# Gated heads of a two-layer decoder step: sample states in a buffer of their own, updates in groups, norm and gates in the next head

## What is computed

```python
def gla_step(s, q, k, v, la):
    bcum = jnp.cumsum(la, axis=1)
    qt = q * jnp.exp(bcum)
    kt = k * jnp.exp(-bcum)
    a = jnp.where(causal, jnp.einsum('bqhd,bshd->bhqs', qt, kt), 0.0)
    o = jnp.einsum('bhqs,bshe->bqhe', a, v) + jnp.einsum('bqhd,bhde->bqhe', qt, s)
    blast = bcum[:, -1]
    k_dec = k * jnp.exp(blast[:, None] - bcum)
    s_new = jnp.exp(blast)[..., None] * s + jnp.einsum('bshd,bshe->bhde', k_dec, v)
    return s_new, o
...
    ob = rms_norm(ob, gla_g).astype(x.dtype).reshape(b, length, W_B)
    mixed = jnp.concatenate([oa * jax.nn.silu(ga), ob * jax.nn.silu(gb)], axis=-1)
```

## Time and profile before

| | us |
|---|---|
| median of 3 runs | 3133.46 (3132.65 to 3137.24) |
| the profiled execution | 3134.93 |
| its span, first to last instruction | 3133.4 |
| PE busy in it | 2939.4 (94%) |
| DVE busy | 1125.1 (36%) |
| ACT busy | 870.7 (28%) |
| DMA queues, mean | 141 GB/s |

### The profile page before, as it was taken

The page is one execution under the profiler, slowest core; times in us unless marked ns, Lnnn a source line. Parts: engine busy times, 40 slices in busy tenths (PEclk is TensorE's granted clock), DMA queues, the critical chain, the costliest instruction groups (busy, mean ns, idle before and its releaser), DMA issues.

```text
span 3133.4 us, 52698 instructions
## 1 busy us (share of the span) xinstructions
PE 2939.4 (94%) x22412; PEld 2712.8 (87%) x22412; DVE 1125.1 (36%) x1589; ACT 870.7 (28%) x1353; POOL 239.3 (8%) x386
## 2 busy tenths in 40 slices
PE   4599997988989898999999999999999999999998
PEld 3388886977978898989899898989989898899998
DVE  1244442232232535334234342433434243443422
ACT  1244343232321322223223132322313232221221
POOL 1020000000000000001010100101010010110111
PEclk7699997988989999999999999999999999999999
DMA  9954431645655343434252533425253443565442
GB/s 308 306 172 123 127 115 43 202 147 155 197 153 160 117 132 108 119 118 150 88 169 83 181 91 119 150 81 174 84 172 96 128 138 104 171 188 168 114 134 65
DMA packets 525769, 442.64 MB, mean 141 GB/s; under 512 B 12320, under 2 KB 491958, under 8 KB 525025
## 3 DMA queue, kind: packets, MB, share of 16 engines
q1 hardware_dynamic: 485664, 300.30, 33.5%
q0 software_dynamic: 39920, 139.52, 12.8%
HBM read 370.39 MB, written 72.51 MB: 141 GB/s over the span
## 4 chain that ended last, share of the span: by engine, by line
PE 86%; DMA 5%; DVE 4%; ACT 2%; issue 1%; POOL 0%; SPq 0%; DVEq 0%; ACTq 0%; POOLq 0%
PE PJ L1458 65%; PE AD L1506 3%; DMA W_raw<-in_ada_w_even 2%; PE X L1440 2%; PE X L1902 2%; PE X L1896 2%; PE PJ L1477 1%; PE X L1869 1%; PE X L1847 1%; PE X L1838 1%; PE X L1477 1%; DMA work<-in_state_gla 1%; DMA out<-work 1%; PE X L1499 1%; PE PJ L1493 1%
## 5 line engine op out<-in xcount | busy, mean ns | idle before, releaser
L1458 PE MATMUL PJ<-act_hi,W_hi 128*128 128x272 f32 x5600 | 1637.1, 292 | 10.2 <-issue 7.3
L1458 PE MATMUL PJ<-act_lo,W_hi 128*128 128x272 f32 x5600 | 1619.2, 289 | 0.0
L1458 PE MATMUL PJ<-act_hi,W_lo 128*128 128x272 f32 x5600 | 1618.2, 289 | 0.0
L1458 PEld LDWEIGHTS PJ<-act_hi,W_hi 128*128 128x128 f32 x5600 | 1061.5, 190 | 47.8 <-issue 41.5
L1458 PEld LDWEIGHTS PJ<-act_lo,W_hi 128*128 128x128 f32 x5600 | 1061.5, 190 | 2.7
L1458 PEld LDWEIGHTS PJ<-act_hi,W_lo 128*128 128x128 f32 x5600 | 1059.2, 189 | 0.0
L997 DVE TENSOR_TENSOR W_lo<-W_raw,W_hi 128x2048 fp32r<-128x2048 f32 x183 | 419.1, 2290 | 488.3 <-ACT W_hi L603 487.7
L603 ACT ACTIVATE W_hi<-W_raw 128x2048 fp32r<-128x2048 f32 x183 | 349.0, 1907 | 249.0 <-PE PJ L1458 231.6
L619 ACT ACTIVATE tiles<-PJ 128x272 f32<-128x272 f32 x222 | 88.2, 397 | 1048.2 <-PE PJ L1458 1033.8
L1355 DVE SCALAR_TENSOR_TENSOR W_raw<-W_raw,work,X 128x512 f32<-128x512 f32 x128 | 90.0, 744 | 144.1 <-PE X L1847 144.1
L1506 PE MATMUL AD<-W_raw,cs 128*32 128x256 f32 x1280 | 93.8, 443 | 27.4 <-DMA W_raw<-in_ada_w_even 27.4
(11 more groups left out here) (355 smaller groups left out, 2579.6 us busy)
## 6 DMA issues: line engine op xcount, KB each, us to landing
W_raw<-in_w_in_odd SPq DMA_DIRECT2D x96, 1024.0 KB, 6.1
W_raw<-in_ada_w_even SPq DMA_DIRECT2D x24, 2048.0 KB, 8.8
W_raw<-in_ada_w_odd SPq DMA_DIRECT2D x24, 2048.0 KB, 8.3
W_raw<-in_w_in_even SPq DMA_DIRECT2D x42, 1024.0 KB, 11.3
W_raw<-in_state_ret POOLq DMA_DIRECT2D x64, 512.0 KB, 7.2
out<-W_raw POOLq DMA_DIRECT2D x64, 512.0 KB, 3.2
W_raw<-in_w_out_odd SPq DMA_DIRECT2D x32, 1024.0 KB, 6.4
W_raw<-in_w_out_even SPq DMA_DIRECT2D x16, 1024.0 KB, 6.2
```

The costliest lines, as they stand in the source:

```text
L1458: last = mm(PJ[:, c, 0:HALF], w[:, par, k], x[:, k, c * HALF:(c + 1) * HALF], start=(k == 0 and a == 0), stop=(k == KT - 1 and a == 2))
```

## The change

- The sample states get a buffer of their own (`SST`, in the upper quarter of `W_raw`). POOL loads the states of the next head as soon as those of this one are stored, and no longer stores, waits and loads between the prompt's and the samples' part.
- The modulation slab keeps the other quarter: 1 MB (`hslab`). It is loaded twice per product, its first half used before the product's first half, its second between the product's halves. A new semaphore `ad_half` tells SP when the first is used. The select moves into the middle of the product's second half.
- Sample outputs (`sample_rows`) stand after the first quarter of the sixth product, the prompt's outputs after the second, and the state products in two groups of four after the third and the fourth. There are four mask buffers, and each PSUM bank takes two products. DVE masks and updates by fours; the last four updates and the sum of squares (`gla_tail`) come in the next head.
- The norm's sum (`gla_norm`) is taken after the first quarter of the next head's first product, or inside the paired product of the output projection behind the last head; the root (`gla_rstd`) and the gates follow there. The first sigmoid is made during the sixth product, the second in the next head. PE no longer waits for the root.
- ACT makes the high part of the next head's second weight at the end of a head; DVE copies the low-rank weights one head ahead.
- The loops of the output projections and of retention heads 1 to 7 are written out on all engines. The modulation loop at the start stays.

```diff
-        BVS, BKM = STK[0:3 * NS, 0:256], STK[0:3 * NS, 512:768].rearrange("p (a b) -> p a b", a=2)
+        BVS, BKM = STK[0:3 * NS, 0:256], STK[0:3 * NS, 256:768].rearrange("p (a b) -> p a b", a=4)
+        hslab = WR[:, 4096:6144].rearrange("p (k n) -> p k n", k=8)
+        SST = WR[:, 6144:8192].rearrange("p (b e) -> p b e", b=NB)
+        N1 = u(5512, T)
...
-                for j in range(6):
-                    load(h * 6 + (N_B + j), (N_B + j) % 2, wie[:, :, src[j]])
-                    ada_pair(h * 6 + (24 + j), ao, h * 1536 + 256 * j)
...
+            gla_weight(0)
+            for i in range(6 * HB):
+                if i + 1 < 6 * HB:
+                    gla_weight(i + 1)
+                else:
+                    load(N_W0, N_W0 % 2, woe[:, :, 0:128])
+
+                sp.wait_ge(s["ad_done"], 24 + i)
+                sp.dma_start(hslab, ao[:, 0:8, 256 * i:256 * i + 256]).then_inc(adl[1], 16)
+                sp.wait_ge(s["ad_half"], i + 1)
+                sp.dma_start(hslab, ao[:, 8:16, 256 * i:256 * i + 256]).then_inc(adl[1], 16)
...
-                wait_for(s["b_o"], h * 2 + 2)
-                pool.dma_start(ST, I["state_gla"][0][:, ds(h, 1)].rearrange("b h p e -> p (b h) e")).then_inc(s["b_sld"], 16)
-                wait_for(s["b_sup"], h * 8 + 8)
-                pool.dma_start(O[8][0][:, ds(h, 1)].rearrange("b h p e -> p (b h) e"), ST).then_inc(s["b_stf"], 16)
-                wait_for(s["b_stf"], h * 16 + 16, "b_free")
+                if h > 0:
+                    pool.wait_ge(s["b_stf"], 16 * h)
+                pool.dma_start(SST, I["state_gla"][0][:, h:h + 1].rearrange("b h p e -> p (b h) e")).then_inc(s["b_sld"], 16)
+                pool.wait_ge(s["b_st"], 8 * h + 8)
+                pool.dma_start(O[4][0, 0, h:h + 1].rearrange("h p e -> p (h e)"), ST[:, 7]).then_inc(s["b_pst"], 16)
+                pool.wait_ge(s["b_sup"], 8 * h + 8)
+                pool.dma_start(O[8][0][:, h:h + 1].rearrange("b h p e -> p (b h) e"), SST).then_inc(s["b_stf"], 16)
...
+            def gla_rstd(h):
+                act.wait_ge(s["b_ms"], h + 1)
+                link(A(halves(N1), X[:, 2:4, 0:HALF], ACT.Ln, bias=eps[:, 0:1], scale=1.0 / 256))
+                A(N1, N1, ACT.Exp, scale=-0.5).then_inc(s["b_rb"], 1)
...
+                gla_evac(4, R3[:, 8 + 2 * h])
+                gla_sigmoid(h, 0)
+                evac(n + 5, 0, R3[:, 9 + 2 * h, 0:HALF])
+                act.wait_ge(s["b_so"], h + 1)
...
+                evac(n + 5, 1, R3[:, 9 + 2 * h, HALF:T])
+                split_hi(n + 7, 0)
...
+                        if k == 2:
+                            gla_sigmoid(HB - 1, 1)
+                        if k == 5:
+                            gla_rstd(HB - 1)
...
+            def gla_silu(h, e):
+
+                dve.wait_ge(s["b_eg"], 2 * h + e + 1)
+                g = R3[:, 8 + 2 * h + e]
+                TT(g, g, T1, ALU.mult).then_inc(s["b_gate"], 1)
+
+            def gla_gate(h):
+
+                dve.wait_ge(s["b_rb"], 3 * h + 3)
+                for e in range(2):
+                    g = R3[:, 8 + 2 * h + e]
+                    link(STT(BP[:, 2 + e], BP[:, 2 + e], vecT2[:, 16 + e:17 + e], N1, ALU.mult, ALU.mult))
+                    dve.wait_ge(s["b_gate"], 4 * h + 2)
+                    TT(g, g, BP[:, 2 + e], ALU.mult).then_inc(s["b_gate"], 1)
...
+            def masked_keys(h, b0):
+                for b in range(b0, b0 + 4):
+                    TS(BKM[:, b % 4], BKS, bmask[0:3 * NS, b:b + 1], None, ALU.mult).then_inc(s["b_kdm"], 1)
+
+            def new_states(h, b0):
+                for b in range(b0, b0 + 4):
+                    at = 256 * (b % 4 // 2)
+                    STT(SST[:, b], SST[:, b], ebl[:, 8 + b:9 + b], X[:, 2 + b % 2, at:at + 256], ALU.mult, ALU.add).then_inc(s["b_sup"], 1)
+
+            def gla_tail(h):
+
+                dve.wait_ge(s["b_ssb"], 8 * h + 8)
+                new_states(h, 4)
+                dve.wait_ge(s["b_rb"], h * 3 + 2)
+                TT(N1, N1, sq1, ALU.add).then_inc(s["b_sq1"], 1)
...
+                    gla_tail(h - 1)
+                    split_lo(n + 1, 0)
+                    gla_silu(h - 1, 1)
...
+                    gla_gate(h - 1)
+                gla_ada(h, 0)
...
+                gla_silu(h, 0)
+                if h + 1 < HB:
+                    dve.wait_ge(s["b_so"], h + 1)
+                    low_rank_weights(h + 1)
+                dve.wait_ge(s["b_ssb"], 8 * h + 4)
+                masked_keys(h, 4)
+                new_states(h, 0)
+                gla_ada(h, 5)
...
+            def ada_rows_half(f):
+                for k in range(8 * f, 8 * f + 8):
+                    g = 32 * (k % 4)
+                    last = mm(AD[g:g + 32, 0:256], cs[:, 9 * k:9 * k + 32], hslab[:, k - 8 * f], start=(k < 4), stop=(k >= KT - 4),
+                              tile_position=(0, g))
+                last.then_inc(s["ad_done" if f else "ad_half"], 1)
+
+            def gla_norm(h):
+                pe.wait_ge(s["b_sq1"], h + 1)
+                pe.wait_ge(s["b_sup"], 8 * h + 8)
+                sum_rows(ones[:, :], N1, banks=(2, 3)).then_inc(s["b_ms"], 1)
...
+                def product_ada(j, quarters=(nothing, nothing, nothing, nothing)):
+                    unit = h * 6 + 24 + j
+                    pe.wait_ge(s["ad_ev"], unit)
+                    pe.wait_ge(adl[1], 32 * (unit - 24) + 272)
+                    ada_rows_half(0)
+                    product_half(n + j, (N_B + j) % 2, 0, between=quarters[0:2])
+                    pe.wait_ge(adl[1], 32 * (unit - 24) + 288)
+                    ada_rows_half(1)
+
+                    def select_and():
+                        ada_select(unit + 1, arow, AD)
+                        quarters[2]()
+
+                    product_half(n + j, (N_B + j) % 2, 1, between=[select_and, quarters[3]])
...
+                def sample_rows():
+                    pe.wait_ge(s["b_sld"], h * 16 + 16)
+                    for e in range(2):
+                        ec = slice(128 * e, 128 * e + 128)
+                        mm(X[:, 4, NS * e:NS * e + NS], VTBs[0:NS, ec], ATs[0:NS], start=True, stop=False)
+                        for b in range(NB):
+                            last = mm(X[:, 4, NS * e + NQ * b:NS * e + NQ * b + NQ], SST[:, b, ec],
+                                      BP[:, 0, SEQ + NQ * b:SEQ + NQ * b + NQ], start=False, stop=(b == NB - 1))
+                    last.then_inc(s["b_so"], 1)
...
-                    pe.wait_ge(s["b_kdm"], h * 8 + (b + 1))
-                    if b >= 2:
-                        pe.wait_ge(s["b_sup"], h * 8 + (b - 1))
-                    mm(X[:, 2 + b % 2, 0:256], BKM[:, b % 2], BVS, start=True, stop=True).then_inc(s["b_ssb"], 1)
-                pe.wait_ge(s["b_sq1"], h * 1 + 1)
-                sum_rows(ones[:, :], T1).then_inc(s["b_ms"], 1)
-                pe.wait_ge(s["b_rb"], h * 3 + 3)
-                pe.wait_ge(s["b_sup"], h * 8 + 8)
+                def state_products(b0):
+                    pe.wait_ge(s["b_kdm"], h * 8 + b0 + 4)
+                    if b0 > 0:
+                        pe.wait_ge(s["b_sup"], h * 8 + b0)
+                    for b in range(b0, b0 + 4):
+                        at = 256 * (b % 4 // 2)
+                        mm(X[:, 2 + b % 2, at:at + 256], BKM[:, b % 4], BVS, start=True, stop=True).then_inc(s["b_ssb"], 1)
+
+                product_ada(5, (sample_rows, prompt_rows, lambda: state_products(0), lambda: state_products(4)))
...
-                    product_pair(base, p0, ready, (X[:, 0], X[:, 1]))
+                    product_pair(base, p0, ready, (X[:, 0], X[:, 1]), beside=(lambda: gla_norm(HB - 1)) if w == 0 else None)
...
-            with pe.Fori(1, HC) as h:
+            for h in range(1, HC):
```

More of the change, by code:

```diff
@@ L488, in out_product @@
                         reload(q)
-                with pool.Fori(start, KT // 2 - 1) as m:
+                for m in range(start, KT // 2 - 1):
                     steps(m)
@@ L556, in _ @@
             head_transfers(0, True, False)
-            with pool.Fori(1, HC - 1) as h:
+            for h in range(1, HC - 1):
                 head_transfers(h, False, False)
@@ L814, in gla_head @@
+                for rows in (KDTs[0:NS], BKS[0:NS], BKS[NS:2 * NS], BKM[0:NS, 0]):
+                    A(rows, X[0:NS, 3, 0:128], ACT.Copy).then_inc(s["b_kta"], 1)
+                gla_evac(3, BP[:, 3])
+                act.wait_ge(s["b_vt"], h + 1)
                 A(VTB.rearrange("p (x a) e -> p x (a e)", x=2), X[:, 0:2, :], ACT.Copy).then_inc(s["b_vta"], 1)
@@ L874, in out_product @@
                 tiles(1, second=True)
-                with act.Fori(2, KT // 2 - 1) as m:
+                for m in range(2, KT // 2 - 1):
                     tiles(m)
@@ L976, in _ @@
             retention_head(0, True)
-            with act.Fori(1, HC) as h:
-                link.loop(h - 1, 8)
+            for h in range(1, HC):
                 retention_head(h, False)
-                link.end(HC - 1)
```

(17 more changed lines are left out.)

226 lines of the change are left out of this document (101 added, 125 removed).

## The result

The changed kernel took 3081.26 us (median of four runs, 3078.06 to 3084.97) where the kernel before took 3134.49 (four runs, 3132.65 to 3137.24): a ratio of 0.983, 95% interval 0.9813 to 0.9847. The forecast was 3078.4. The profiled execution took 3084.97 (span 3083.2), 49.96 less than the 3134.93 of the one before; the sum of the prediction gave 56.5.

What follows compares the result with a forecast made beforehand. TensorE work, 86% of the chain of waits, was taken as the bound, so only its idle or half-clock time could be won. 75.7 us won less 19.2 lost gave 56.5 net: 3134.9 - 56.5 = 3078.4, range 3051 to 3113.

Steps and rivals of the forecast that it cites:

- Three transitions: Between gated heads, PE's remaining work is 9.6 us each, replacing transitions of 27.2, 25.4 and 26.9 us: gain 50.7 us.
- Last transition: From head 3 to the output projection, 25.9 us shrinks to 12.6, with 6.2 on DVE's path: gain 13.3 us.
- Select: In gated products, PE's 0.50 us wait before the select goes as it moves 3 us later: gain 2.0 us.
- Loops: Written-out retention loops lose the 7.3 us of back-edge gaps and some half-clock time: gain 9.0 us.
- Rival (d): Written-out loops bring nothing because straight code waits at the same place: 3087 us, chance 0.05.
- Breaks: Slab in two halves and pieces inside products interrupt PE's product stream more often: cost 6.6 us.
- Half slabs without waits: In gated products, each 1 MB half slab lands in 5.8 us, before PE needs it: no wait.
- (b): Half slab and weight share the DMA engines; second halves 2.4 us late in 24 products: 3135 us, chance 0.05.
- (c): Second half slabs land as late as a weight beside POOL's traffic, 6.5 us late 24 times: 3234 us, chance 0.08.
- Collisions: POOL's state store and load delay half slabs at the start of heads 1 to 3: cost 6.0 us.
- Clock: One half-clock stretch of 1.65 us per gated head, with the sample rows inside a product: cost 6.6 us.
- Rival (a): Hand-over inside the product shows: state products at 0.39 us, a second half-clock stretch per head: 3093 us, chance 0.10.

## Why the prediction was right, term by term

The forecast time is 2.9 us off the median, 6.6 off the profiled execution, and inside its range. That it is so close is partly luck. The terms of the gated part sum to 47.5, and it gave 34.6 (505.65 to 471.05); the loops gave 16.4 in place of 9.0 and made up for more than half of that. The path and the mechanisms held; the sizes of three terms did not.

- *Three transitions, 50.7: held.* PE's own work was put at 9.6 a head. At full clock it is 4.4 for the sample rows (two blocks of 1.88 and two of 0.34), 1.05 for the state products (0.58 + 0.47; 1.0 assumed from the earlier trace rows against the 0.39 of the earlier trace rows), 0.92 for the norm, 1.4 for the low-rank product, 2.0 for the slab: 9.8. The wait for the states' DMA is gone.
- *Last transition, 6.2 us behind the product: held.* From the product's end at 990.28 to the paired product at 996.06 it is 5.8 us: the second group of state products 0.49, then DVE as described (updates 1.66, sum 0.63, low part 2.20). The product pair behind it took 1.3 us more, which contains the norm at 0.92.
- *Select, 2.0: held.* It takes 0.34 with no wait ahead of it, where the earlier trace rows had 0.50 of waiting and 0.61.
- *Loops, 9.0: the size failed.* 16.4 in this pair, 17.8 over thirteen executions. The step took the gaps, 7.3, and 1.7 for the half-clock stretches behind them; the rest of these it left in place, because the loop's entry has such a stretch without a gap. Written out, 32 of 60 boundaries are at full clock, with a loop one of 18. Rival (d) is dead.
- *Breaks, 6.6: near.* 24 x 0.32 = 7.7, of which two blocks of slab rows carry most.
- *Half slabs without waits: held.* A landing of 5.4 against 5.8, and no wait in head 0 nor behind the third product of the others. Rivals (b) and (c) needed 8.4 and 8.6. One reading behind this term was wrong: the slab of the earlier trace rows did not travel alone. The trace of the kernel before has another slab of 2 MB ahead of it until 84.46 us and a further one issued behind it at 88.18, before it landed at 90.58, so the two equal landing times show nothing. The conclusion stands by the changed kernel: in head 0 the half slabs with a weight issued 0.4 us behind landed in 5.19 to 5.47, those without in 5.09 to 5.26 but for one of 6.59. The 6.15 us for 1 MB that the prediction had from the Trainium skill, "DMA: Bandwidth & Descriptors", section "Measured (HBM→SBUF, 128 partitions, SWDGE, issued from GpSimd)", was too long for this queue; the measurement decides.
- *Collisions, 6.0: the largest miss.* The mechanism and its place were right, but the waits cost 11.8, or 3.9 a head, the very end of the bound that was worked out (0 to 3.9); the 2 that was taken rested on no row. The second half came 1.09, 0 and 1.06 late (1.7 was the bound), the next first half 3.05, 2.95 and 3.24 (2.2). And a stall of about 3 us can have a tail, the half clock behind it (5.01 for 3.2, 1.93 for 1.00); it did in heads 2 and 3, 5.4 together, and not in head 1. That makes 17.2, where the kernel that loads the states once gained 17.4 in the gated part. The one with the states in pieces gained 14.0 there and 11.5 in time; its profiled execution lost 1.7 more behind the sample rows than the changed kernel's first.
- *Clock, 6.6: too small.* By the chain of the changed kernel it was 9.3; rows in blocks that leave the clock alone gained 11.7 in time. The price was taken from one half-clock stretch at the retention entry; here a part of the rows themselves can run at 1.2 GHz as well (3.50 for 1.88 in head 1).

With the measured sizes the sum is 56.5 + 7.4 (loops) - 1.1 (breaks) - 11.2 (collisions) - 2.7 (clock), all by the traces of the pair, = 48.9 against 49.96; the last 1.1 us are not assigned. Rival (a), the hand-over that shows, fell: DVE's turns stayed covered, and the second half-clock stretch in each head that its 3093 had would have made the clock 13.2, where it cost 9.3.

What stays open: why a boundary between written-out retention heads is at full clock in one execution and not in another, why one stall of 3 us is followed by half clock and another not, what the clock gate reads in the sample rows, and whether the size or the moment of POOL's transfers made the half slabs late.

## What to carry to other kernels

Price a gap on TensorE together with the half-clock stretch behind it: at the back edges here it brought as much as the gap (8.0 and 7.1 us), and it followed two of three DMA stalls of 3 us too. When a buffer is halved until its load has half a product to land, look at what every other queue issues in that very window; the remedy is to move or cut that other traffic, which kept its 2 MB a head here and lost the six waits but for 0.3 us. Small matmuls that must run on TensorE did best here in short blocks between long streams, neither in two blocks of sixteen instructions nor mixed singly into the stream.

## What the runs showed of the hardware that was not expected

- A written-out boundary has no gap at all, while a loop on PE alone costs as much as loops on all engines: 3101.86 against 3098.99 (0.9892 and 0.9884 of the kernel before on the same chip), and 3081.26 (0.983) without.
- The clock fell to 1.2 GHz in a mix of product matmuls and 4-column products without a pause, and stayed there through the rest of the mix and the prompt rows, with PE busy 16.45 of 16.45 us. The same small products in blocks of about 1 us between quarters of 3.1 us stayed at 1.00.
- 1 MB in pieces twice as long as a weight's landed in 5.4 us on SP's queue, against 6.1 for a weight and 8.3 for the 2 MB slab in the kernel before.
